# Expert outputs stored row by row and fetched at the end, and an opening with the first weight unit split in quarters

## What is computed

```python
def chunk_gmlp(x, norm_g, w_in, b_in, ...):            # layer 0, the opening of the kernel
    h = rmsnorm(x, norm_g)
    z = gelu(h @ w_in + b_in)                          # w_in: 1024 x 4096
    u, v = z[..., :2048], z[..., 2048:]
    ...

def moe_swiglu(h, w_router, wg, wu, wd):               # layer 1, the end of the kernel
    t = h.reshape(-1, 1024)
    probs = softmax(t @ w_router)                      # 8 experts
    top_p, top_i = lax.top_k(probs, 2)
    top_p = top_p / sum(top_p)
    gates = sum(one_hot(top_i, 8) * top_p[..., None], axis=-2)
    def expert(acc, xs):
        wg_e, wu_e, wd_e, g_e = xs
        y = (silu(t @ wg_e) * (t @ wu_e)) @ wd_e       # inner width 2816
        return acc + g_e[:, None] * y, None
    ...

x = x + mla_mixer(...)                                 # layer 1
x = x + moe_swiglu(rmsnorm(x, f_norm_g[1]), ...)       # y_prompt, y_sample
```

## Time and profile before

| what | us |
|---|---|
| median of 3 runs (lowest, highest) | 1825.77 (1823.91, 1826.25) |
| the profiled execution | 1823.55 |
| its span | 1821.9 |
| TensorE busy | 1730.2 (95%) |
| VectorE busy | 1278.5 (70%) |
| ScalarE busy | 970.7 (53%) |
| GpSimd busy | 74.5 (4%) |
| chain that ended last: TensorE, VectorE, ScalarE | 80%, 11%, 4% |

### The profile page before, as it was taken

One profiled execution on the slowest core, in us unless ns is written; L12 is line 12 of the kernel. 1 busy time (PEld: TensorE's weight loads), 2 busy tenths in 40 slices (PEclk: granted clock), 3 DMA queues, 4 the chain that ended last, 5 costly groups with the idle time before them and its releaser, 6 DMA issues.

```text
span 1821.9 us, 25052 instructions
## 1 busy us (share of the span) xinstructions
PE 1730.2 (95%) x8926; PEld 1442.5 (79%) x8926; DVE 1278.5 (70%) x1696; ACT 970.7 (53%) x1211; POOL 74.5 (4%) x141
## 2 busy tenths in 40 slices
PE   6999999999988899999996999999999999999997
PEld 5698989999865767777775888888888888888885
DVE  5467365553378575556538889898898989898995
ACT  4344243332344454444333667676867677676763
POOL 0000000000001102211100000000000000000000
PEclk8999999999999999999997999999999999999998
DMA  8342433334322101100014889898989989888982
GB/s 303 116 150 73 159 117 139 139 138 145 110 102 76 30 0 44 44 29 29 29 59 162 311 335 361 326 374 303 374 327 342 349 332 352 334 353 324 381 321 109
DMA packets 71469, 368.91 MB, mean 202 GB/s; under 512 B 8240, under 2 KB 18752, under 8 KB 34336
## 3 DMA queue, kind: packets, MB, share of 16 engines
q1 hardware_dynamic: 64256, 351.82, 51.5%
q0 software_dynamic: 5408, 11.43, 2.1%
q10 hardware_dynamic: 1728, 4.63, 0.7%
HBM read 365.61 MB, written 2.24 MB: 202 GB/s over the span
## 4 chain that ended last, share of the span: by engine, by line
PE 80%; DVE 11%; issue 4%; ACT 4%; DMA 1%; DVEq 0%; ACTq 0%; SPq 0%; PEldq 0%
PE bank L1538 24%; PE bank L1540 23%; PE bank L1539 23%; PE bank L1821 2%; PE bank L1975 1%; PE bank L1957 1%; ACT at_r L812 1%; PE bank L1983 1%; DVE sks L1227 1%; ACT at L772 1%; PE bank L1741 1%; PE bank L1630 1%; DVE rs_t L927 1%; DVE rs_t L928 1%; DVE at_r L1402 0%
## 5 line engine op out<-in xcount | busy, mean ns | idle before, releaser
L1538 PE MATMUL bank<-at_r,at_r 128*128 128x512 f32 (+3 forms) x2076 | 760.2, 366 | 26.9 <-PE bank L1540 9.2
L1540 PE MATMUL bank<-at_r,at_r 128*128 128x512 f32 (+3 forms) x2076 | 747.2, 360 | 0.0
L1539 PE MATMUL bank<-at_r,at_r 128*128 128x512 f32 (+3 forms) x2076 | 746.6, 360 | 0.0
L1306 DVE TENSOR_TENSOR at_r<-at,at_r 128x2048 fp32r<-128x2048 f32 x264 | 597.0, 2289 | 73.1 <-ACT at_r L812 69.1
L812 ACT ACTIVATE at_r<-at 128x2048 fp32r<-128x2048 f32 x264 | 496.2, 1913 | 1.6 <-PE bank L1540 1.6
L1538 PEld LDWEIGHTS bank<-at_r,at_r 128*128 128x128 f32 (+1 forms) x2076 | 387.3, 187 | 88.9 <-issue 16.9
L1540 PEld LDWEIGHTS bank<-at_r,at_r 128*128 128x128 f32 (+1 forms) x2076 | 387.2, 187 | 55.0
L1539 PEld LDWEIGHTS bank<-at_r,at_r 128*128 128x128 f32 (+1 forms) x2076 | 387.9, 187 | 50.3
L938 DVE TENSOR_TENSOR at_r<-at,at_r 128x2048 fp32r<-128x2048 f32 x57 | 130.4, 2289 | 103.6 <-ACT at_r L569 103.5
L569 ACT ACTIVATE at_r<-at 128x2048 fp32r<-128x2048 f32 x57 | 108.9, 1913 | 132.3 <-PE bank L1540 92.9
L1227 DVE TENSOR_REDUCE sks<-at 128x8 f32<-128x1024 f32 x64 | 77.9, 1216 | 79.0 <-ACT at L772 79.0
(11 more groups left out here) (314 smaller groups left out, 1450.3 us busy)
## 6 DMA issues: line engine op xcount, KB each, us to landing
at<-in_m_un SPq DMA_DIRECT2D x264, 1024.0 KB, 4.8
at<-in_d_gu SPq DMA_DIRECT2D x22, 1024.0 KB, 4.9
at<-in_w_in SPq DMA_DIRECT2D x16, 1024.0 KB, 6.0
at<-in_d_down SPq DMA_DIRECT2D x11, 1024.0 KB, 5.0
at<-in_w_out SPq DMA_DIRECT2D x8, 1024.0 KB, 5.0
at<-in_c_lat POOLq DMA_DIRECT2D x64, 128.0 KB, 2.3
at<-in_w_o SPq DMA_DIRECT2D x2, 2048.0 KB, 10.1
at<-in_w_uq SPq DMA_DIRECT2D x2, 1152.0 KB, 10.6
```

The source lines that it names most:

```text
L1306: TT(low_part[raw_slot[q]], raw[raw_slot[q]], high_part[hi_slot[q]].bitcast(f32), SUB).then_inc(u_lo, 1)
L1538: mm(out, xh, wh, start=first, stop=False)
L1539: mm(out, xh, wl, start=False, stop=False)
L1540: return mm(out, xl, wh, start=False, stop=last)
```

## The change

It has two parts.

**Expert results.** `SelT`, the gates per slot (`gatec`, `gslot`, `item_gate`), `y_low`, `scatter_mm` and `scatter_out` go. ScalarE copies an expert's result without a gate and stores it, 128 rows of 1024, in a new buffer in device memory, `expert_rows` (`y_rows`), on its own queue; the next pass's copy waits for that store. Each token's two gates stay in `top_gate`, and the numbers of its two rows in `row_i`, which VectorE works out behind the first gather. POOL clears the rows of the four possible further passes ahead of pass 0. After the last pass ScalarE waits for the last store, reads the number of further passes and tells POOL. POOL issues six fetches by index, two for each tile, into `y_of`, and VectorE adds them to `X` with the gates as factors, two operations a tile. SP stores each tile of `X` as it is done.

**Opening.** A small Gelu on ScalarE comes first, so that the table load stands there. Unit 0's copy comes ahead of the eight columns. VectorE makes unit 0's low part in four quarters of 512, each followed by one column split, and the first by a residual column. TensorE's first product of each of the four k of tile 0 waits for that column alone. The semaphores `c_new` and `kr_new` become one.

```diff
-        SelT = area(34, NTOK, r=True)
-        ygp = (area(94.5, D_MODEL, r=True), area(98.5, D_MODEL, r=True))
+        top_gate = area(105.25, 2, NT)
+        row_i = sb("row_i", [P, 2 * NT], i32)
+        y_rows = nc.dram_tensor("expert_rows", (NITEM * P, D_MODEL), f32, kind="Internal").ap()
+        y_of = (area(82.5, NT, D_MODEL), area(60.5, NT, D_MODEL))
...
         @block.sync
-            sp.wait_ge(x_ready[4], 1)
             for t in range(NT):
+                sp.wait_ge(x_ready[4], t + 1)
...
         @block.gpsimd
+            pool.wait_ge(s_zero, 3)
+            pool.memset(yg, 0.0).then_inc(s_zero, 1)
+            pool.wait_ge(s_zero, 4)
+            for o in range(MAX_EXTRA):
+                pool.dma_start(y_rows[(N_EXPERTS + o) * P:(N_EXPERTS + o + 1) * P, :], yg).then_inc(y_zero, 16)
+            pool.wait_ge(all_stored, 1)
+            for t in range(NT):
+                for c in range(2):
+                    R = slice(0, ROWS[t])
+                    pool.indirect_dma_start(y_of[c][R, t, :], None, y_rows[:, :],
+                                            bass.IndirectOffsetOnAxis(ap=row_i[R, NT * c + t:NT * c + t + 1], axis=0))\
+                        .then_inc(y_back[t], 16)
...
         @block.scalar
+            A(rs_t[0:1, 0:1], G[0:1, 0:1], ACT.Gelu_apprx_tanh)
+            ahead(0)
             for k in range(KC):
                 act.wait_ge(ntr, k + 1)
                 A(hTp[0][:, k, :], bank[k][:, 0:NTOK], ACT.Copy, scale=G[:, G_A + k:G_A + k + 1]).then_inc(n_hi, 1)
-                if k == 3:
-                    ahead(0)
...
+                if isinstance(e, int) and e == 0:
+                    act.wait_ge(y_zero, 16 * MAX_EXTRA)
+                else:
+                    act.wait_ge(y_stored, 16 * e)
                 for hf in range(2):
-                    A(yg[:, hf * 512:(hf + 1) * 512], bank[hf][:, :], ACT.Copy, scale=gslot[:, 0:1]).then_inc(y_done, 1)
...
+                    A(yg[:, hf * 512:(hf + 1) * 512], bank[hf][:, :], ACT.Copy).then_inc(y_done, 1)
+                act.wait_ge(y_done, 2 * e + 2)
+                act.dma_start(rows, yg).then_inc(y_stored, 16)
...
         @block.vector
+            dve.wait_ge(u_hi, 1)
+            for k in range(4):
+                c = slice(512 * k, 512 * k + 512)
+                i = TT(low_part[0][:, c], raw[0][:, c], dense_high_part[0][:, c].bitcast(f32), SUB)
+                if k == 3:
+                    i.then_inc(u_lo, 1)
+                columns_low(k, bank[k][:, 0:NTOK])
+                if k == 0:
+                    keep(0)
...
-            link(TT(g3(T0), g3(O1), b3(2), MUL))
-            link(TT(g3(T1), g3(O2), b3(4), MUL))
-            link(TT(g(T0), g(T0), g(T1), ADD))
-            link(TT(g3(GA), g3(T0), b3(6), MUL))
+            for c in range(2):
+                TT(top_gate[:, c, :], c3(2 + 2 * c), c3(6), MUL)
...
+            for t in range(NT):
+                R = slice(0, ROWS[t])
+                dve.wait_ge(y_back[t], 32)
+                STT(X[R, t, :], y_of[0][R, t, :], top_gate[R, 0, t:t + 1], X[R, t, :], MUL, ADD).then_inc(y_added, 1)
+                dve.wait_ge(y_added, t + 1)
+                STT(X[R, t, :], y_of[1][R, t, :], top_gate[R, 1, t:t + 1], X[R, t, :], MUL, ADD).then_inc(x_ready[4], 1)
...
         @block.tensor
-                            pe.wait_ge(n_lo, max(4, o + 1))
+                            pe.wait_ge(n_lo, min(8, o + 1))
                             pe.wait_ge(x_new, o + 1)
...
                         for k in range(4):
+                            if o == 0 and h == 0:
+                                pe.wait_ge(n_lo, k + 1)
...
-                    if j in SCATTER_AT and prev:
-                        scatter_mm(e - 1, SCATTER_AT[j])
-                    if j == SELECT_AT:
-                        if prev:
-                            pe.wait_ge(sc_done, 6 * e)
-                        for t in range(NT):
-                            R = slice(0, ROWS[t])
-                            T(bank[6][:, tok(t)], Sel[R, t, :].bitcast(f32), ident[R, R])
-                        for t in range(NT):
-                            R = slice(0, ROWS[t])
-                            i = mm(bank[7][:, 0:1], Sel[R, t, :].bitcast(f32), gatec[R, t:t + 1], start=(t == 0), stop=(t == 2))
-                        i.then_inc(selT_mm, 1)
```

More of the change, by code:

```diff
@@ L358, in dense_slots, with in_order @@
             return n % ND_RAW, n % ND_HI
-        def in_order(step):
-            done = [0]
+        def in_order(step, done=None):
+            done = [0] if done is None else done
             def ahead(n):
@@ L877, in pass_act @@
                 wait_last(act, unit_used, e, NU - 1)
[L878 to L880 removed]
+                if isinstance(e, int) and e == 0:
+                    act.wait_ge(y_zero, 16 * MAX_EXTRA)
+                else:
+                    act.wait_ge(y_stored, 16 * e)
                 for hf in range(2):
[L882 to L885 removed]
+                    A(yg[:, hf * 512:(hf + 1) * 512], bank[hf][:, :], ACT.Copy).then_inc(y_done, 1)
+                act.wait_ge(y_done, 2 * e + 2)
+                rows = y_rows[e * P:(e + 1) * P, :] if isinstance(e, int) else y_rows[bass.ds(e * P, P), :]
+                act.dma_start(rows, yg).then_inc(y_stored, 16)
             prologue(0, 2)
@@ L893, in _ @@
             over_passes(act, pass_act)
+            act.wait_ge(y_stored, 16 * N_EXPERTS)
             def act_further(i):
@@ L993, in _, with keep @@
             dve.wait_ge(s_zero, 1)
-            for half in range(2):
-                ks = range(4 * half, 4 * half + 4)
-                for k in ks:
-                    columns_low(k, bank[k][:, 0:NTOK])
-                for k in ks:
-                    TS(xT[:, k, :], bank[k][:, 0:NTOK], G[:, G_BO + k:G_BO + k + 1], None, ADD).then_inc(x_new, 1)
-                ahead(half)
+            def keep(k):
+                TS(xT[:, k, :], bank[k][:, 0:NTOK], G[:, G_BO + k:G_BO + k + 1], None, ADD).then_inc(x_new, 1)
+            dve.wait_ge(u_hi, 1)
[7 more added lines that the diff above has]
+                    keep(0)
+            first_unit[0] = 1
+            for k in range(1, 4):
+                keep(k)
+            for k in range(4, 8):
+                columns_low(k, bank[k][:, 0:NTOK])
+            ahead(1)
+            for k in range(4, 8):
+                keep(k)
             dve.wait_ge(nsq, 3)
@@ L1540, in products, with dense_unit @@
                 return mm(out, xl, wh, start=False, stop=last)
-            def dense_unit(n, chunks):
-                pe.wait_ge(u_lo, n + 1)
+            def dense_unit(n, chunks, first=False):
+                if not first:
+                    pe.wait_ge(u_lo, n + 1)
                 i, h = dense_slots(n)
@@ L1579, in _ @@
                 for h in range(2):
-                    w = dense_unit(2 * n + h, 4)
+                    w = dense_unit(2 * n + h, 4, first=n == 0 and h == 0)
                     for t in range(NT):
@@ L1966, in gather_tr @@
                     i.then_inc(gt_mm, 1)
-            def scatter_mm(e, steps=range(6)):
-                pe.wait_ge(y_lo, 2 * e + 2)
-                for n in steps:
-                    t, hf = n // 2, n % 2
-                    if n >= 2:
-                        pe.wait_ge(sc_done, 6 * e + n - 1)
-                    for part in range(2):
-                        i = mm(bank[6 + hf][0:ROWS[t], :], SelT[:, tok(t)], ygp[part][:, hf * 512:(hf + 1) * 512],
-                               start=(part == 0), stop=(part == 1))
-                    i.then_inc(sc_mm, 1)
             def h_tr(e, j):
```

107 lines of the change are left out of this document (41 added, 66 removed).

## The result

The kernel after takes 1799.05 us (median of 4 runs, 1795.60 to 1800.11), the kernel before, beside it, 1824.84 (1822.13 to 1826.25): ratio 0.9858, 95% interval 0.9844 to 0.9871. The forecast was 1793.5, the range 1787 to 1803. It was faster by the mechanism that was forecast, and 5.5 us later than the forecast.

A forecast was written before the change was run, and what follows sets the result against it. TensorE was taken to bound the eight expert passes, with dependency chains at both ends. Passes -30.7, opening -5.8, routing +0.8 and end +3.5 sum to -32.2 us, forecasting a median of 1793.5 us, range 1787 to 1803.

The forecast's parts named there:

- Passes: Expert passes: scatter (18.9 us in passes 1 to 7) and Sel and gate products (11.8 in eight) leave TensorE, -30.7 us.
- The rival that TensorE would wait for the next selection: Passes: the Sel products' time only covered the wait for the next selection; 11.8 us lost, 1805; 3%.
- The stream rivals: Passes: weight stream becomes the bound at 343 GB/s, 1832 (2%), or binds a little later at 353 GB/s, 1812 (4%).
- Opening: Program start: first product at 13.9 instead of 19.84, unit 0 done earlier; -5.8 us, from 3.9 to 7.2.
- the shift stays: Behind the opening: every load is issued by a freed slot, so the opening's -5.8 us is kept.
- The rival of the eaten opening: Opening: TensorE starts early, but half clock or a unit landing late gives the gain back; 1799; 12%.
- Routing: Around the first gather and pass 0: -0.9 us ahead of the gather, +1.7 for tables; sum +0.8, from -0.9 to +3.
- The tables: VectorE's tables behind the first gather: grow by 16 linked operations, lose 8 linked and 2 loose; +1.7 us, not hidden.
- End: Behind the last pass: store, branch, six fetches by index, adds and last store replace the old chain; +3.5 us.
- the other pairs landing in time: End: first pair of fetches lands 3.3 us after a 1.2 us issue, and VectorE never waits for later pairs.
- The bound of +14: End: rival that each fetch must land before the next is issued, +14 instead of +3.5, 1804; 10%.
- the 1.4 us that I worked out by that page: End: the last two fetches would wait behind VectorE's first adds, about 1.4 us more, an estimate.

The follow-up runs named there:

- tables_spread: Kernel after, with VectorE's tables and row numbers behind the first gather spread over steps 1 to 10 of pass 0; 1791.18 us, ratio 0.9816.
- end_split: Kernel after, with four VectorE subtractions of the weight splits' form beside the fetches at the end; 1800.08 us, one execution.
- end_busy: Kernel after, with six more VectorE operations of the adds' form beside the fetches at the end; 1797.29 us, one execution.
- lower_first: tables_spread with the end rebuilt: rows of each token's lower-numbered expert fetched in pass 7, three fetches left behind the last store; 1784.41 us, ratio 0.9785.
- stream_2: Kernel after, with two more stores of 1 MB, never read back, behind each expert's result; 1805.03 us, one execution, passes 96.84 us apart.

## Why the prediction was right, and where it was off

**Passes, right.** 4.24 us a pass against 4.17. Passes 1 to 7 give 29.6, and the 1.47 of pass 0 is in its balance below: 31.1 for 30.7. What the scatter and the `Sel` products gave one by one was not measured. The rival that TensorE would wait for the next selection did not come. The stream rivals fail at 385 GB/s, and 358, which the Trainium skill gives in "DMA: Bandwidth & Descriptors", section "Where 436 GB/s comes from", is exceeded for two whole passes.

**Opening, right where it was worked out, and then half lost.** The first product (13.94 for 13.9) and unit 0 (5.67 for 5.8) came as written. The step that failed is the last sentence, "the shift stays". I followed the units, and not the clock in the idle times behind. In the profiled execution the fall at 167 us costs 2.7, and another 0.6 goes between the norm at 236 and the router. The fall comes in some executions and not in others. The rival of the eaten opening named half clock at the opening itself; it happened 150 us later. The runs show that it comes and goes with the same instructions; what decides it is open. That idle time lies in front of it is shown; that filling it takes the fall away is likely, on one profile.

**Routing, mis-sized.** Ahead of the first gather it is 0.9 (from -2.30 at the router's transposes to -3.24 at the gather): right. Another 0.5 between the gather and pass 0 was not forecast; the clock is low there for 3.3 us instead of 5.5. The tables were put at +1.7 and cost a wait of 2.95, though on VectorE they grew by only 1.4. The step that failed: I took TensorE to arrive when it did before, when it ended its last product of gate and up at 1010.59, just as VectorE was done. There its first products of pass 0 ran at 1.2 GHz from 1001.2 to 1004.6, which hid 1.7 us of the tables. In the kernel after the fall comes behind the wait, at the same price. So pass 0 loses 2.95, gains the 1.47 of Sel, and is 1.56 longer. tables_spread shows that wait and fall go together: 4.85 us.

**End, mis-sized: +8.2 for +3.5.** From ScalarE's first copy to POOL's first issue it is 6.05 for 5.6. From there to the first pair landed it is 6.6 for 4.5, and the second pair makes VectorE wait 2.33 where nothing was put down. The adds and the last store are as forecast. (The terms as they stand add up to 1825.2, +3.3, and not to 1825.3, +3.5.) The step that failed is the landing: the price of one load of 512 KB at 413 GB/s, with "the other pairs landing in time". All six carry 2.62 MB behind one store, which even at that rate is 6.3 us; I had added 1.0 for one load. In fact the DMA engines are busy from 1780 to 1790, at 244 to 324 GB/s in stretches of 2 us. The bound of +14 named the wrong mechanism (one after the other): issues overlap the transfers, and the bytes queue.

**"DVE blocks DMA".** The Trainium skill, "SBUF — State Buffer", says in the box on that trap that POOL cannot write descriptors while VectorE holds the port they share. I set the page loads of 537 to 558 ns against it. The traces of end_split, end_busy and lower_first agree with the page for fetches by index: an issue that begins inside a VectorE operation waits for its end. Plain loads on the same queue show no such wait. In the kernel after two page loads were issued inside a subtraction of the splits' form, were done before it ended, and took what they take elsewhere:

```profile
569.85 2.28 DVE L1210 TENSOR_TENSOR at_r<-at,at_r 128x2048 fp32r<-128x2048 f32 x1
570.56 0.54 POOL L514 DMA_DIRECT2D at<-in_c_lat  x1 [0.60 <-issue]
571.14 0.54 POOL L516 DMA_DIRECT2D at<-in_c_kr  x1
```

So the page loads were read rightly, but they say nothing about fetches by index. A fetch has a list of rows to read besides; whether that read is what waits was not tried. In the kernel after no fetch's issue began inside a VectorE operation: the sixth began 0.29 us ahead of the first add and took 0.91, so the 1.4 us that I worked out by that page did not come.

**By terms**, spans of the profiled executions, measured for forecast: opening up to the router -2.3 for -5.8; routing and pass 0 +0.1 for -0.7; passes 1 to 7 -29.6 for -29.2; end +8.2 for +3.5; sum -23.6 for -32.2. That the time lies in the range is luck in part. The opening (2.3) and the end (+8.2) both lie outside what was put down for them (3.9 to 7.2, and +2.7 to +8), and the range reached 1803 for a rival that did not come as it was described.

## What to carry to other kernels

Work that leaves the bounding engine pays in full while every other stream has measured room (4.24 us a pass for 4.17 here), and the room can be measured with stores that nobody reads. Where many transfers start together behind one event, the last byte sets the time: add up all bytes, at a rate measured on transfers of the same kind, and look which of them could have gone earlier (half of them here, 6.8 us together with the other changes of lower_first). A gain at the start of a program can be lost again where TensorE's clock falls behind an idle time, and small VectorE work hidden under a slow clock shows up when that slow stretch goes.

## What the runs showed of the hardware that was not expected

POOL's issue of a fetch by index waits for a VectorE operation that runs when it starts: 2.94 us instead of 0.95, with splits of 2.29 us and operations of 1.28 us alike. Two issues that began 0.04 and 0.06 us behind an operation's start did not wait, one that began 0.07 us behind did. A plain load on the same queue does not wait: 0.54 us inside a subtraction of 2.28 us.

Rows of 4 KB on POOL's queue take longer for their bytes than the weight units. In 1780 to 1790 of the kernel after 728 packets of 3.6 KB took 88.6% of 16 engines, 0.19 us each, 18 GB/s an engine. In 1310 to 1340 of stream_2 the weight queue reads

```profile
q1 hardware_dynamic: 1625, 11.87, 94.3%
```

which is 0.28 us for 7.3 KB, 26 GB/s an engine. Whether the size, the queue or the place in memory makes the difference was not tried.

The granted clock differs between executions of one program, and the time with it: of the twelve executions of the opening alone the five shortest (1816.4 to 1817.7 us) have a mean granted clock of 0.984 to 0.985, the other seven (1820.2 to 1825.6) one of 0.981 to 0.984.
